# Four placings moved in a hand-ordered transformer block: values in their own unit, index pieces in four runs, a ring of four output weights, a nested loop for experts' further blocks

## The chip, the cores and the metric

The kernel runs on one core of one Trainium2 chip. The metric is the device time of one execution in microseconds (us). The engines are TensorE (PE in the profile, its weight loads PEld), VectorE (DVE), ScalarE (ACT), GpSimd (POOL) and SyncE (SP, which here only issues DMAs).

## What is computed

One layer of a streaming encoder over 1024 tokens of 1024 features, in float32. A mixer (an indexer that picks 256 keys for sparse attention, beside a forgetting attention), then a mixture of 32 experts, each behind an adaLN norm, then a last norm. Cut to what matters:

```python
x = x + gate1(c) * Mixers(adaLN(rmsnorm(x), c))
x = x + gate2(c) * HierMoE(adaLN(rmsnorm(x), c))
return rmsnorm(x, g_final)

# Mixers
rel   = einsum('bqhd,bsd->bqhs', qi_blk, ki) * IDX_SCALE        # index scores, 8 heads
score = einsum('bqh,bqhs->bqs', wi_blk, relu(rel)); sel = top_k(score, 256)
oa = softmax(q . k[sel]) . v[sel]                               # branch a, one shared key head
ob = softmax(q . k + cum_q - cum_k) . v                         # branch b, causal
merged = sigmoid(ga) * (oa @ w_out_a) + sigmoid(gb) * (ob @ w_out_b)
return merged @ w_out

# HierMoE: every token goes to 2 of 32 experts; an expert's tokens are padded to blocks of 128
hid = silu(xb @ w_e_gate[e]) * (xb @ w_e_up[e])                 # 1024 -> 512
y_block = hid @ w_e_down[e]                                     # 512 -> 1024
```

With the inputs of this case the 32 experts have, in the order in which the kernel takes them, 1,1,1,2,1,1,3,2,2,1,2,1,1,1,7,3,1,1,2,2,1,1,3,1,1,1,1,1,2,1,1,1 blocks: 51 in all. Here they are called expert 0 to expert 31 in that order.

## The kernel before

The program of each engine is written out by hand, in the order in which it runs; engines meet by semaphores only. The stages, with their place in the profiled execution: norms and the first projection (to 131 us), the index scores (131 to 206), the rest of the gate columns of that projection (206 to 545), 64 attention units (555 to 794), the output weights of the two branches (795 to 900), the merged projection, the second norm and the router (900 to 1050), the experts (1050 to 1773), the last norm (to 1809).

A product that needs more than one pass of rounded numbers is written as three matmuls (L1192, L1193, L1194), each operand being split into a rounded high part (by ACT) and what is left (by DVE).

Index scores: 24 pairs of heads' scores (L1186); ACT turns each score tile into its relu (`positive`, L891), DVE adds it to the block's sum (L1691, L1694) and thereby frees one of two relu buffers. Between the pairs PE does 32 pieces of the gate columns, three matmuls each, placed by the table `PIECE_AFTER` after 21 of the pairs, never more than four in a row. In the stage before, DVE has, at its steps t=6 and t=7, two `mod_sums` (L1547), which multiply rows of the modulation.

Attention: unit n is a pair of heads by a block of 128 queries. On PE a turn of the loop does `turn_p(n)` (transposes of unit n's probabilities, L1328), the scores of unit n+3 (L1315), and `values(n-1)` (L1340): the values of a unit come a turn behind its transposes. ACT copies the transposes out of the accumulators (`turned`, L943), which `values` waits for; DVE's `out` (L1790) copies the result out, takes the largest score (L1771) and scales (L1785).

Output weights: 16 units u, each 24 matmuls against a slice of `w_out_a` and `w_out_b`. SP loads the slice (L591), ACT rounds it (L953), DVE makes its rest (L1866) and merges the results (L1910, L1912). There are two buffers for the slices, and SP issues the load of slice u when PE is through with slice u-2.

Experts: `expert()` is written five times, once ahead of a loop, three times in it and once behind. The loop runs ten times over three experts; in this text place 1, 2 and 3 are the three experts of a turn, so that place 3 is followed by the loop's jump back (L1521). The number of an expert's blocks is read at run time: its first block stands unconditional, the second and third behind a compare-and-branch each (L1505, L1507), the rest behind a third (L1509). Behind that one there are two copies of the block's program, each within a loop: one for blocks 3 to 7, one for blocks 8 up. `MORE` is where the second begins. Expert 14 alone has more than three blocks.

Of the kernel before, what the change touches and what calls it, by code (L numbers as in the profile page):

```python
# [45 lines left out]
MORE = 8  # L46
# [27 lines left out]
PIECE_AFTER = [0, 0, 0, 0, 1, 1, 2, 2, 5, 6, 6, 7, 8, 9, 10, 10, 11, 12, 13, 13, 14, 15, 16, 16, 17, 18, 19, 19, 20, 21, 22, 22]  # L74
# [65 lines left out]
def build(nc, x, c, positions, w_mod, b_mod, g_mix, w_in, b_forget, w_out_a, w_out_b, w_out, g_ffn,  # L140
# [13 lines left out]
    with ExitStack() as ctx:  # L154
# [85 lines left out]
        relu = [at(30, U), at(31, U)]  # L240
# [65 lines left out]
        w_raw = [at(u, U) for u in (13, 28)]  # L306
        w_lo = [fr(u, U) for u in (13, 28)]
        w_hi = [fr(u, U) for u in (34, 35)]
# [71 lines left out]
        wo_in = [sem(f"wo_in{z}") for z in range(2)]  # L380
# [26 lines left out]
        sq2_ok = sem("sq2_ok")  # L407
        ms2_ok = sem("ms2_ok")
        sqrt2_ok = sem("sqrt2_ok")
# [101 lines left out]
        def _(sp):  # L511
# [44 lines left out]
            bias_rows(0)  # L556
            for j in range(2):
                sp.wait_ge(gate_ok, 2 * j + 2)
                gate_store(0, j)
            for s in GATE_SLOTS:  # L560
# [27 lines left out]
            def weights_o(u):  # L588
                m, z = u % KT, u % 2
# [15 lines left out]
            for u in range(2):  # L605
                weights_o(u)
# [3 lines left out]
            for u in range(4):  # L610
                gates_back(u)
            for u in range(2, N_G):
                if u >= 4:
                    sp.wait_ge(mg_done, 2 + u - 3)
                    gates_back(u)
                sp.wait_ge(yab_ps, u - 1)
                weights_o(u)
                if u == KT + 2:
                    weights_out(0)
# [36 lines left out]
            sp.wait_ge(sq2_ok, TT)  # L656
# [28 lines left out]
        def _(pool):  # L685
# [57 lines left out]
            pool.wait_ge(sq2_ok, TT)  # L743
# [60 lines left out]
        def _(act):  # L804
# [80 lines left out]
            def positive(n):  # L885
                w = WB[B0 + n // NH]
                act.wait_ge(rel_ps, n + 1)
                if n >= 2:
                    act.wait_ge(score_ok, n - 1)
                b = 2 * (n % 3)  # L890
                act.activation(relu[n % 2][:, 0:w], ps[:, b:b + 2, :].rearrange("p a b -> p (a b)")[:, 0:w], ACT.Relu,  # L891
# [59 lines left out]
            def high_w(u):  # L951
                act.wait_ge(wo_in[u % 2], 32 * (u // 2) + 32)
                act.activation(w_hi[u % 2], w_raw[u % 2], ACT.Copy).then_inc(whi_ok, 1)  # L953

            for n in range(N_IU):
                positive(n)
                for g in range(4):
                    if n == 2 * PIECE_AFTER[KT * g + KT - 1] + 1 + (g > 0):
                        gate_half(g)
                if n in (24, 26):  # L960
                    high_slot(1, (n - 24) // 2)
# [69 lines left out]
            for t in range(TT + 1):  # L1031
# [3 lines left out]
                if t < TT:  # L1035
                    act.wait_ge(x1_ok, 2 * t + 2)
                    if t >= 1:
                        act.wait_ge(sq2_ok, t)
                    act.activation(sqj, x1[t], ACT.Square, accum_out=ssq[:, t:t + 1]).then_inc(sq2_ok, 1)
                    act.wait_ge(ms2_ok, t + 1)  # L1040
                    act.activation(rstd[:, t:t + 1], ssq[:, t:t + 1], ACT.Sqrt).then_inc(sqrt2_ok, 1)
# [52 lines left out]
            for t in range(TT):  # L1094
                act.wait_ge(x_in[t], 48)
                if t >= 1:
                    act.wait_ge(sq2_ok, TT + t)
                act.activation(sqj, xf[t], ACT.Square, accum_out=ssq[:, t:t + 1]).then_inc(sq2_ok, 1)
                act.wait_ge(ms2_ok, TT + t + 1)
                act.activation(rstd[:, t:t + 1], ssq[:, t:t + 1], ACT.Sqrt).then_inc(sqrt2_ok, 1)  # L1100

        @block.tensor
        def _(pe):
# [116 lines left out]
            for k in range(SCORE_PAIRS):  # L1220
                index_scores(2 * k)
                for i, after in enumerate(PIECE_AFTER):
                    if after == k:
                        piece(i // KT, i % KT)
# [4 lines left out]
                if k == 3:  # L1229
# [130 lines left out]
            for n in range(-LEAD, N_U + 1):  # L1360
                groups = len(key_groups(n)) if 0 <= n < N_U else 0
# [8 lines left out]
                if n >= 1:  # L1370
                    for f in range(len(key_groups(n - 1))):
# [757 lines left out]
```

## Time and profile before

| | us |
|---|---|
| median of 3 runs | 1813.42 (1812.15 to 1817.22) |
| profiled execution | 1810.58, of it the span 1808.8 |
| experts, 1050 to 1773 | 723.0, PE busy 610.8 |
| output weights, 795.1 to 900.4 | 105.3, PE busy 93.7 |
| index scores, 131.4 to 206.1 | 74.7, PE busy 63.8, DVE busy 55.2 |
| attention, 555 to 794 | 239.0, PE busy 220.2 |

The page adds up busy time by engine and by line over the whole span. The waits and the timeline tell which idle time lies ahead of which line and what ended it; "issue" is idle time in which the engine waited for nothing that the profile shows. The chain of waits follows the end of the program back, so that idle time in it is time that the program is long by.

### The profile page before, as it was taken

Reading aid. Unit: us, or ns where it says so; the run is one execution under the profiler, and the core shown is the slowest. Engines: PE = TensorE matmul, PEld = TensorE weight load, DVE = VectorE, ACT = ScalarE, POOL = GpSimd, SP = SyncE. Lnnn points to the kernel's source line nnn. Section 1 sums busy time; section 2 is a strip of 40 time slices with the busy share of each in tenths; the row PEclk is TensorE's granted clock in tenths of the full one; section 3 lists DMA queues with packets and bytes.
Section 4 is the critical chain, followed back from the end, with each engine's and each line's share of the span. In section 5 each row is a group of like instructions: output and inputs, shape, how many; then the busy total and the mean of one; then the engine's idle time right before and its main releaser. Section 6 shows DMA issues by size and latency. Waiting matters only on the chain.

```text
span 1808.8 us, 23911 instructions
## 1 busy us (share of the span) xinstructions
PE 1573.7 (87%) x8440; PEld 946.8 (52%) x8441; DVE 846.9 (47%) x1981; ACT 504.7 (28%) x1011; POOL 206.9 (11%) x372
## 2 busy tenths in 40 slices
PE   6989999999999999989799578898969989696693
PEld 3554578898897666667688432333323323232231
DVE  6887877877796777856565611111101111010013
ACT  4335421122225767742312111111101111010012
POOL 1110000000001210000000022222212222221121
PEclk9999999999999999999999788999989999898896
DMA  9651023321110002025661689868892588868955
GB/s 356 222 185 60 24 86 101 94 59 47 47 47 24 25 2 82 1 82 183 199 215 70 259 334 370 343 229 297 312 359 56 172 300 319 337 220 324 405 206 192
DMA packets 122316, 327.68 MB, mean 181 GB/s; under 512 B 14814, under 2 KB 64006, under 8 KB 97570
## 3 DMA queue, kind: packets, MB, share of 16 engines
q1 hardware_dynamic: 110404, 308.36, 45.9%
q0 software_dynamic: 11744, 16.82, 4.3%
q8 instruction: 137, 2.24, 0.6%
q14 instruction: 31, 0.25, 0.0%
HBM read 301.74 MB, written 34.39 MB: 186 GB/s over the span
## 4 chain that ended last, share of the span: by engine, by line
PE 80%; issue 8%; DVE 7%; DMA 2%; ACT 2%; SPq 1%; POOL 0%; POOLq 0%; ACTq 0%; DVEq 0%
PE ps L1457 22%; PE ps L1192 10%; PE ps L1475 9%; PE ps L1194 9%; PE ps L1193 9%; PE ps L1315 3%; PE ps L1328 3%; PE ps L1150 3%; PE ps L1340 3%; DVE arena L1771 2%; PE ps L1186 2%; DMA arena<-in_w_mod_dram 1%; PE ps L1451 1%; PE ps L1153 1%; PE ps L1466 1%
## 5 line engine op out<-in xcount | busy, mean ns | idle before, releaser
L1457 PE MATMUL ps<-arena 128*64 128x512 f32 x1632 | 400.1, 635 | 112.9 <-issue 112.2
L1457 PEld LDWEIGHTS ps<-arena 128*64 128x64 f32 x1632 | 123.4, 145 | 346.5 <-issue 339.6
L2073 DVE TENSOR_TENSOR arena<-arena,ps 128x256 f32<-128x256 f32 x51 | 21.5, 421 | 532.1 <-ACT arena L1066 532.1
L1475 PE MATMUL ps<-arena 128*64 128x512 f32 x816 | 183.8, 592 | 0.6 <-DVE arena L2089 0.6
L1716 DVE TENSOR_SCALAR_CACHE_REDUCE arena<-arena,small 128x384 bf16<-128x384 f32 (+2 forms) x192 | 169.3, 942 | 0.0
L1070 ACT ACTIVATE arena<-ps 128x256 f32<-128x256 f32 x51 | 19.5, 383 | 441.6 <-PE ps L1466 441.6
L796 POOL DMA_INDIRECT sum_rows<-arena,ones x51 | 81.5, 1598 | 531.7 <-DVE arena L2089 508.6
L1192 PE MATMUL ps<-rounded_quad,rounded_pair 128*128 128x512 f32 x352 | 138.2, 393 | 2.5 <-ACT arena L891 2.5
L1194 PE MATMUL ps<-rounded_quad,rounded_pair 128*128 128x512 f32 x352 | 137.1, 390 | 0.0
L1193 PE MATMUL ps<-rounded_quad,rounded_pair 128*128 128x512 f32 x352 | 137.1, 390 | 0.0
L1771 DVE CUSTOM_DVE_ANT_0 arena<-ps,arena 128x896 f32<-128x896 f32 (+7 forms) x128 | 91.8, 755 | 66.6 <-PE ps L1315 66.0
L1475 PEld LDWEIGHTS ps<-arena 128*64 128x64 f32 x816 | 58.7, 137 | 116.5 <-issue 116.5
L1192 PE MATMUL ps<-rounded 128*128 128x512 f32 x256 | 103.8, 405 | 17.1 <-issue 11.5
L936 ACT ACTIVATE arena<-arena,small 128x896 f32<-128x896 f32 (+7 forms) x128 | 98.5, 774 | 57.7 <-DVE small L1771 57.2
L1193 PE MATMUL ps<-rounded 128*128 128x512 f32 x256 | 101.9, 398 | 0.0
L1194 PE MATMUL ps<-rounded 128*128 128x512 f32 x256 | 101.8, 398 | 0.0
L2089 DVE SCALAR_TENSOR_TENSOR arena<-ps,ones,arena 128x512 f32<-128x512 f32 x51 | 38.3, 751 | 115.8 <-PE ps L1475 115.8
L1315 PE MATMUL ps<-arena 64*128 64x512 f32 (+3 forms) x384 | 79.3, 517 | 7.1 <-DVE small L1771 7.0
L1328 PE MATMUL ps<-ident,arena 128*128 128x128 f32 x576 | 80.2, 280 | 4.3 <-ACT arena L943 3.5
L1340 PE MATMUL ps<-arena 128*64 128x128 f32 x1152 | 77.0, 278 | 7.2 <-DVE arena L1790 6.2
L737 POOL TENSOR_SCALAR_AFFINE_SELECT arena<-arena 128x128 f32<-128x128 f32 x64 | 24.8, 413 | 508.5 <-DVE small L1771 478.4
L943 ACT ACTIVATE arena<-ps 128x512 f32<-128x512 f32 (+1 forms) x160 | 77.8, 549 | 12.8 <-PE ps L1328 12.8
(313 smaller groups left out, 2426.3 us busy)
## 6 DMA issues: line engine op xcount, KB each, us to landing
arena<-in_w_e_up_dram SPq DMA_DIRECT2D x64, 1024.0 KB, 11.9
arena<-in_w_e_gate_dram SPq DMA_DIRECT2D x64, 1024.0 KB, 10.2
arena<-in_w_e_down_dram SPq DMA_DIRECT2D x32, 2048.0 KB, 9.3
arena<-in_w_mod_dram SPq DMA_DIRECT2D x12, 2048.0 KB, 8.7
plain_pair<-in_w_in_dram SPq DMA_DIRECT2D x30, 512.0 KB, 5.2
arena<-in_x_dram SPq DMA_DIRECT2D x16, 512.0 KB, 7.3
gate_rows<-arena SPq DMA_DIRECT2D x16, 512.0 KB, 2.8
arena<-gate_rows SPq DMA_DIRECT2D x32, 256.0 KB, 4.3
```

The lines of the kernel that those rows point to most:

```text
L796: pool.indirect_dma_start(y_q, bass.IndirectOffsetOnAxis(idx_s[q][:, 0:1], 0), ye[z], None, bounds_check=S * NT - 1, oob_is_err=False, com ...
L936: act.activation(buf, buf, ACT.Exp, bias=nmax[:, u:u + 1], scale=-1.0, accum_out=rs[:, u:u + 1]).then_inc(p_done, 1)
L1192: pe.matmul(out, w_h, a_h, start=first, stop=False)
L1193: pe.matmul(out, w_h, a_l, start=False, stop=False)
L1194: return pe.matmul(out, w_l, a_h, start=False, stop=last)
L1315: m = pe.matmul(ps[:, 2 * z + a // 512, 0:e - a], q[half, b * P:(b + 1) * P], k[half, a:e], start=True, stop=True)
L1328: m = pe.transpose(ps[:, turn_bank(k), (2 * i + z) * P:(2 * i + z + 1) * P], lg[n % 4][z][:, kb * P:(kb + 1) * P], ident[:])
L1340: m = pe.matmul(ps[z * HD:(z + 1) * HD, 6, 0:P], v, pT[k % PT][:, (2 * i + z) * P:(2 * i + z + 1) * P], start=kb == 0, stop=kb == b)
L1457: m = pe.matmul(ps[o * TB:(o + 1) * TB, 2, 0:2 * FQ].rearrange("p (j n) -> p j n", j=2), xT[:, k % NX, k // NX * TB:(k // NX + 1) * TB], w ...
L1475: m = pe.matmul(ps[o * TB:(o + 1) * TB, 5, 0:DQ], hidT[:, k % NH_T, k // NH_T * TB:(k // NH_T + 1) * TB], w_dn[c][:, k, o * DQ:(o + 1) * D ...
L1716: chain.up(dve.tensor_scalar(junk[b % 2][:, 0:WB[B0 + b]], scb[b], thr(b), None, op, ALU.add, accum_out=cnt[:, b:b + 1]))
L1771: dve.tensor_tensor_reduce(lg[n % 4][z][:, 0:w], ps[:, 2 * z:2 * z + 2, :].rearrange("p a n -> p (a n)")[:, 0:w], added, -1.0 if kind == " ...
```

## The change

It does these things:

- Attention: `values` of unit n come in unit n's own turn, behind the scores of unit n+3; DVE's `out` moves with them.
- Index scores: the 32 pieces stand in four runs of eight, after pairs 2, 9, 14 and 19. A third relu buffer. The two `mod_sums` stand between scores of this stage (after scores 5 and 19). Small steps (transposes of the cumulative sum, rounding of slot 1) come later in the stage, and SP's `bias_rows(0)` waits for the stage's end.
- Output weights: a ring of four buffers for slices. Slice 0 is loaded before the attention ends, 1 to 3 behind its last scores (before: slices 0 and 1 ahead of them), and slice u when PE is through with slice u-4.
- Experts: behind the third compare-and-branch one copy of the block's program in a nested loop in the place of two.
- Six semaphores become three, with counts that go on.

```diff
-MORE = 8
+MORE = 5
-PIECE_AFTER = [0, 0, 0, 0, 1, 1, 2, 2, 5, 6, 6, 7, 8, 9, 10, 10, 11, 12, 13, 13, 14, 15, 16, 16, 17, 18, 19, 19, 20, 21, 22, 22]
+PIECE_AFTER = (2, 9, 14, 19)
-        relu = [at(30, U), at(31, U)]
+        relu = [at(30, U), at(31, U), at(35, U)]
-        w_raw = [at(u, U) for u in (13, 28)]
-        w_lo = [fr(u, U) for u in (13, 28)]
-        w_hi = [fr(u, U) for u in (34, 35)]
+        w_raw = [at(u, U) for u in (13, 9, 12, 28)]
+        w_lo = [fr(u, U) for u in (13, 9, 12, 28)]
+        w_hi = [fr(u, U) for u in (14, 36, 34, 35)]
...
-            for u in range(2):
-                weights_o(u)
+            weights_o(0)
             for z in range(2):
                 sp.wait_ge(gate_out[z], 16 * KT)
             sp.wait_ge(lg_done, 2 * N_U)
             for u in range(4):
+                if u >= 1:
+                    weights_o(u)
                 gates_back(u)
-            for u in range(2, N_G):
-                if u >= 4:
-                    sp.wait_ge(mg_done, 2 + u - 3)
-                    gates_back(u)
-                sp.wait_ge(yab_ps, u - 1)
+            for u in range(4, N_G):
+                sp.wait_ge(yab_ps, u - 3)
                 weights_o(u)
+                sp.wait_ge(mg_done, 2 + u - 3)
+                gates_back(u)
...
             def positive(n):
                 act.wait_ge(rel_ps, n + 1)
-                if n >= 2:
-                    act.wait_ge(score_ok, n - 1)
+                if n == 2:
+                    act.wait_ge(k_spread, TT)
+                if n >= 3:
+                    act.wait_ge(score_ok, n - 2)
...
-                if n in (24, 26):
-                    high_slot(1, (n - 24) // 2)
+                if n in (33, 35):
+                    high_slot(1, (n - 33) // 2)
...
             for k in range(SCORE_PAIRS):
                 index_scores(2 * k)
-                for i, after in enumerate(PIECE_AFTER):
-                    if after == k:
-                        piece(i // KT, i % KT)
+                for g in range(4):
+                    if PIECE_AFTER[g] == k:
+                        for kt in range(KT):
+                            piece(g, kt)
...
-            for n in range(-LEAD, N_U + 1):
-                groups = len(key_groups(n)) if 0 <= n < N_U else 0
+            for n in range(-LEAD, N_U):
+                groups = len(key_groups(n)) if n >= 0 else 0
...
-                if n >= 1:
-                    for f in range(len(key_groups(n - 1))):
-                        values(n - 1, f)
+                for f in range(groups):
+                    values(n, f)
...
                 with pe.If(3 < blocks):
-                    with pe.Fori(3, MORE) as k:
-                        with pe.If(k < blocks):
-                            token_block(first + k, c, own)
-                    with pe.If(MORE < blocks):
-                        with pe.Fori(MORE, RUN) as k:
-                            with pe.If(k < blocks):
-                                token_block(first + k, c, own)
+                    with pe.Fori(0, (RUN - 3 + MORE - 1) // MORE) as far:
+                        with pe.If(3 + MORE * far < blocks):
+                            with pe.Fori(0, MORE) as k:
+                                with pe.If(3 + MORE * far + k < blocks):
+                                    token_block(first + 3 + MORE * far + k, c, own)
...
                 low_h(t)
-                mod_sums(4 + t)
+                if t < TT - 2:
+                    mod_sums(4 + t)
...
+                for g in range(2):
+                    if n == 2 * PIECE_AFTER[g] + 1:
+                        mod_sums(10 + g)
...
-            for n in range(-LEAD, N_U + 2):
-                if n >= 2:
-                    out(n - 2)
+            for n in range(-LEAD, N_U + 1):
+                if n >= 1:
+                    out(n - 1)
```

On PE, the end of an expert's program before, from the third compare-and-branch (L1509) to the end of the second copy of a block:

```order
L1509 COMPARE_AND_BRANCH
L1510 UNCONDITIONAL_BRANCH
L1511 COMPARE_AND_BRANCH
L1481 ISA
L1457 MATMUL ps<-arena 64x512 x8
L1466 MATMUL ps<-ident,arena 128x128 x2
L1448 REGISTER_ALU
L1451 MATMUL ps<-ident,arena 128x128 x4
L1457 MATMUL ps<-arena 64x512 x8
L1475 MATMUL ps<-arena 64x512 x8
L1511 UNCONDITIONAL_BRANCH
L1510 REGISTER_ALU
```

And after, where the same branch stands on L1509 again:

```order
L1509 COMPARE_AND_BRANCH
L1510 UNCONDITIONAL_BRANCH
L1510 ISA
L1511 COMPARE_AND_BRANCH
L1512 UNCONDITIONAL_BRANCH
L1512 ISA
L1513 COMPARE_AND_BRANCH
L1481 ISA
L1457 MATMUL ps<-arena 64x512 x8
L1466 MATMUL ps<-ident,arena 128x128 x2
L1448 REGISTER_ALU
L1451 MATMUL ps<-ident,arena 128x128 x4
```

Before, these rows are followed by a second copy of the block (L1515); after, by the ends of the two loops and the next expert's reads of its numbers (L1501). So the branch jumps over one copy, not two.

On PE, the turn of an attention unit before, with the transposes (L1328), the scores (L1315) and the values (L1340):

```order
L1328 MATMUL ps<-ident,arena 128x128 x12
L1315 MATMUL ps<-arena 128x512 x2
L1328 MATMUL ps<-ident,arena 128x128 x2
L1340 MATMUL ps<-arena 64x128 x16
L1328 MATMUL ps<-ident,arena 128x128 x12
L1315 MATMUL ps<-arena 128x384 x2
```

After, in the same place (L1329, L1316 and L1341 are the same lines, moved by one):

```order
L1329 MATMUL ps<-ident,arena 128x128 x12
L1316 MATMUL ps<-arena 128x512 x2
L1329 MATMUL ps<-ident,arena 128x128 x2
L1341 MATMUL ps<-arena 64x128 x14
L1329 MATMUL ps<-ident,arena 128x128 x12
L1316 MATMUL ps<-arena 128x384 x2
```

The 16 matmuls belong to the unit before, the 14 to the unit whose 14 transposes stand above them.

On SP, the loads of the output weights (L591) among the gates' (L597) before:

```order
L591 DMA arena<-in_w_out_a_dram 128x4x128
L591 DMA arena<-in_w_out_b_dram 128x4x128
L591 DMA arena<-in_w_out_a_dram 128x4x128
L591 DMA arena<-in_w_out_b_dram 128x4x128
L597 DMA arena<-gate_rows 128x512 x8
L591 DMA arena<-in_w_out_a_dram 128x4x128
```

After, each slice has its gates behind it:

```order
L589 DMA arena<-in_w_out_a_dram 128x4x128
L589 DMA arena<-in_w_out_b_dram 128x4x128
L595 DMA arena<-gate_rows 128x512 x2
L589 DMA arena<-in_w_out_a_dram 128x4x128
L589 DMA arena<-in_w_out_b_dram 128x4x128
L595 DMA arena<-gate_rows 128x512 x2
```

## Rows read from the trace of the kernel before

**Rows 1.** The page: the span of the profiled execution.

```profile
span 1808.8 us, 23911 instructions
```

**Rows 2.** Stretches: bounds, length, busy (x) of PE PEld DVE ACT POOL, clock, DMA share, GB/s.

```profile
1050.00:1773.00 723.00, 610.81 (x2736) 221.31 (x2736) 79.72 (x151) 92.11 (x205) 151.81 (x198) 0.94 0.76 281
795.10:900.40 105.30, 93.68 (x384) 74.45 (x384) 56.98 (x77) 28.52 (x41) 0.00 (x0) 0.95 0.54 170
131.40:206.10 74.70, 63.77 (x269) 32.58 (x269) 55.22 (x72) 44.77 (x63) 1.02 (x2) 0.93 0.14 41
555.00:794.00 239.00, 220.19 (x2096) 153.83 (x2095) 171.25 (x503) 174.10 (x414) 21.28 (x56) 1.00 0.11 34
240.00:480.00 240.00, 240.00 (x1240) 203.49 (x1239) 191.55 (x521) 47.85 (x62) 0.00 (x0) 1.00 0.24 71
```

**Rows 3.** Waits of PE, 1040 to 1790 us: total, times, longest.

```profile
PE ps L1457 <- issue: 112.2, 29, 11.8
```

**Rows 4.** The chain of waits, its pieces of idle time: start us, us, what.

```profile
1088.24 3.63 issue
...
1252.93 6.72 issue
...
1310.28 11.20 issue
...
1567.95 11.77 issue
...
1643.69 11.26 issue
...
1681.65 4.00 issue
...
1698.95 11.25 issue
```

**Rows 5.** Expert 12's branches on PE's queue: count, ns, start.

```profile
L1509 PEldq COMPARE_BRANCH  x1: 5482/5482/5482, 1306.5 to 1306.5; - x1
L1521 PEldq COMPARE_BRANCH  x1: 7347/7347/7347, 1312.2 to 1312.2; - x1
```

**Rows 6.** Timeline of PE: start, us, line, names, count, idle before.

```profile
1298.69 3.65 PE L1457 MATMUL ps<-arena 128*64 128x512 f32 x16 [2.24 <-issue]
1306.67 3.60 PE L1475 MATMUL ps<-arena 128*64 128x512 f32 x16
1321.48 4.97 PE L1457 MATMUL ps<-arena 128*64 128x512 f32 x16 [11.20 <-issue]
```

**Rows 7.** DMA queue of instructions, 240 to 480 us: packets, MB, share.

```profile
q8 instruction: 9, 0.15, 0.3%
```

**Rows 8.** Output weights, 795.1 to 900.4 us: a wait, groups by line, PE's timeline.

```profile
ACT rounded L953 <- DMA arena<-in_w_out_b_dram: 75.8, 14, 11.4
L1192 PE MATMUL ps<-rounded 128*128 128x512 f32 x128 | 52.5, 410 | 13.3 <-issue 11.5 <-DVE rounded L1866 1.7
L1866 DVE TENSOR_TENSOR rounded<-arena,rounded 128x1024 fp32r<-128x1024 f32 x15 | 18.4, 1225 | 33.3 <-ACT rounded L953 33.3
799.34 0.39 PE L1194 MATMUL ps<-rounded 128*128 128x512 f32 x1
...
801.63 0.39 PE L1192 MATMUL ps<-rounded 128*128 128x512 f32 x1
```

**Rows 9.** Index scores, 131.4 to 206.1 us: groups by line, DVE and PE.

```profile
L1694 DVE SCALAR_TENSOR_TENSOR arena<-arena,small 128x384 f32<-128x384 f32 (+5 forms) x42 | 40.0, 951 | 15.1 <-ACT arena L891 12.8
L1547 DVE SCALAR_TENSOR_TENSOR arena<-arena,small 128x512 f32<-128x512 f32 x8 | 6.0, 752 | 0.2
L1192 PE MATMUL ps<-rounded_quad,rounded 128*128 128x512 f32 x32 | 15.7, 491 | 5.8 <-DVE rounded L1635 5.8
```

**Rows 10.** Timeline of attention, unit 38's turn: start, us, engine, line.

```profile
699.16 0.49 PE L1315 MATMUL ps<-arena 64*128 64x128 f32 x4
...
700.13 1.34 ACT L943 ACTIVATE arena<-ps 128x512 f32<-128x512 f32 x3
```

## The prediction before the result

> **What bounds the kernel now.** I read four views, in this order. First the table of stretches [rows 2]. TensorE is what the whole span [rows 1] is made of: in the gate columns it is busy for all 240.00 us of 240.00, so nothing is to be had there. It is not busy all the time in four other stages, and the change touches exactly these: the experts (610.81 of 723.00 us), the output weights (93.68 of 105.30), the index scores (63.77 of 74.70) and the attention (220.19 of 239.00).
>
> Then PE's waits over the experts [rows 3]: 112.2 us in 29 gaps, all ahead of the first gate matmuls of an expert (L1457), and all "issue": no semaphore, no weights. The chain of waits holds these gaps, so the end is late by them. It also shows their size by place in the loop [rows 4]. At 1252.93, 1310.28, 1567.95, 1643.69 and 1698.95 us they are 6.72, 11.20, 11.77, 11.26 and 11.25 us: these five, 52.2 us, stand behind experts with one block at place 3, where the loop jumps back. The rows 3.63 and 4.00 are the first and the last of six at place 2 (20.7 us together). What is left, some 39 us, is small gaps at all places.
>
> The branches say what the gaps are made of. Behind expert 12 the third compare-and-branch takes 5.48 us and the loop's jump 7.35 us [rows 5]; the work that was queued ahead runs on for a part of that, and 11.20 us stay open. Such a branch costs little when it doesn't jump, so it is the fetch of instructions at the target that is paid. The first work behind a long gap is slow too: L1457's first half takes 4.97 us behind the gap of 11.20 and 3.65 us behind one of 2.24 [rows 6].
>
> Last the output weights [rows 8]: ACT waits 75.8 us for the slices' DMA, the slice of DVE's rest (L1866) waits for ACT, and PE has 13.3 us idle ahead of L1192.
>
> **Part D, the nested loop.** It takes one copy of a block out of what the third branch jumps over. How much is that? Nine packets of instructions came in 240 us [rows 7], for 1240 matmuls and 1239 weight loads [rows 2]: some 275 a packet. A block is 54 matmuls and 54 loads, 0.4 packet with its few others. The branch jumped over nearly a whole packet and jumps over half of one now; the turn of three experts shrinks from about 6.8 packets to 5.5. The rows don't show a jump over half a packet. The bounds: it costs as much as today's (nothing gained), or it falls within what is already there and costs nothing; then all that L1509 adds goes. I take half of the branch's 5.48 us, 2.7 us, since every second such jump then ends in a packet that the engine holds. For the jump back I take 7.35 less 2.7, by the same step, for the shorter way. So a long gap at place 3 loses 5.5 us: five times 5.5 is −27.5. At place 2 only the branch bears on it: the six gaps lose half, −10. Where gaps fall from 4 to 2 us the slow first half (4.97 against 3.65 [rows 6], 1.3 us each) goes as well, for some three of them: −4. The small gaps I leave. What stands next behind them is the weights: an expert's are 6.3 MB, and 281 GB/s at a share of 0.76 [rows 2] is 370 GB/s at full share, so 17.0 us an expert against 11.4 us of matmuls for one block (three pieces of 3.6 us as in [rows 6] and the turns between them); 51 blocks take 580 us, 32 experts' weights 545. Over the stage it holds, and three sets are loaded ahead, but strings of one-block experts eat that up. Sum D: −41, from 0 to −55.
>
> By a page of the Trainium skill, "Runtime: NRT & Kernel Launch", section "Instruction fetch mechanics", instructions come in blocks of 256, two of which are held, and a jump out of this window forces a fetch; by that a skip of about one block or of half of one would mostly fall inside, and the gaps at L1509 would not be there. The trace has 5.48 us on such a skip, so it pays well inside of two packets; taken by the rule alone, the shorter skip would bring nothing there, which is the rival of no gain below.
>
> **Part C, the ring of four.** Today SP asks for a slice when PE has done the one two before, so the slice has little over one unit's time (5.4 us: 24 matmuls by the pitch of 0.2267 us that the ten matmuls from 799.34 to 801.63 us show [rows 8]) to land, be rounded by ACT and by DVE (1.2 us). With four it has three units' time, 16 us. The stage then goes at that pitch: 384 by 0.2267 is 87.1 us against 105.3, −18. DVE has 57.0 us of work there [rows 2], no bound. But slice 1 to 3 are asked for only when the last scores are done, all at once beside gates, and land late for units 1 and 2; and the first matmuls stand at the lower clock (mean 0.95). I put +2 for that. Sum C: −16, from −12 to −17. In the last units of attention the earlier slice 1 is missing, but nothing reads it.
>
> **Part B, the index scores.** The pieces were a cover: PE did one or two of them while ACT and DVE worked a pair off. Eight in a row are 24 matmuls, 5.4 us and 0.4 of slower first ones: 5.8 us in which no score comes. The ring of three gives DVE three scores (3 by 0.951 us, 2.9) in them. So DVE stands 2.9 us in each of four runs, 11.6. It also gets 6.3 us more of work: `mod_sums` is 8 by 0.752 us [rows 9] and two now lie between scores, where one had its place at the stage's beginning. 55.2 plus 6.3 of work, 11.6 behind the runs and 8 us of today's 19.5 idle (74.7 less 55.2 [rows 2]) that I keep for the stage's start are 81.1 us, and I round up for the transposes, which now stand between scores too: 82 against 74.7, +7. DVE becomes the bound. Against it works that `mod_sums` covers the first two runs, that PE's wait of 5.8 us on L1635 [rows 9] at the start goes: then +1. If also the covers fail, +9. The stage before stays: PE bounds it. SP's `bias_rows(0)` behind the stage's end has the whole gate stage to land in: nothing.
>
> **Part A, values in their own unit.** Before, a turn lay between the transposes and the values; now only the scores of unit n+3 do. In unit 38's turn PE ends these scores at 699.65 us and ACT's copies of its transposes run to 701.47 [rows 10]: the values would stand 1.8 us. That is where the unit three ahead is short and the unit itself long, once or a little more in each eight units: 8 by 1.8 is 14.6. PE is idle for 18.8 us of the stage already (239.00 less 220.19 [rows 2]), and a wait put in takes half of another's place. So +7, from 0 (the waits only change places) to +15. `out` comes a turn earlier as well, and the stage's last turn is a unit shorter: below 0.5 us.
>
> The merged semaphores add and remove no instruction that waits longer: 0.
>
> **The sum.** Against the profiled execution's 1810.6: −41 −16 +7 +7 is −43, 1767.6. The median of the runs is 2.8 us over the profiled one: 1770.
>
> **Rivals.**
> (1) Only part of D comes. The gaps shorten, but now PE gets to experts before their weights: in strings of one-block experts 17.0 us of transfer stand against 11.4 of work. For it: DMA share 0.76 over the stage, near full in its strings. Against: today no wait of L1457 names a DMA of weight. Half of D, some 20 us, is lost: 1790. I give it 0.22.
> (2) More of D comes. The skip stays within what is held at nearly all places: −41 becomes −55, and the index stage loses only 2: 1751 to 1752. 0.10.
> (3) D brings nothing, since a jump costs a fetch whatever its length; the edit doesn't do in effect what its form says. −16 +7 +7 is −2: 1811. 0.11.
> (4) Slower. Where a jump lands in a packet decides what it costs, as the places show: 11 us at place 3, 2 to 4 at the others, for the same skip. The program's layout shifts, and behind the shorter skip the loops' ends and the next expert's reads fall on a packet's edge at place 2 and 1 as well. If eight gaps there rise from 3.4 to the 6.7 of the smallest long one [rows 4], that is +26, and with −2 for the rest 1835 to 1838. It decides from 0.3 us per gap on. 0.07.
> My forecast, 1760 to 1780, has 0.50.
>
> **The numbers.** Three tenths of a per cent, 5.4 us, is about what a measurement of this kernel can tell from no change. The forecast and rivals 1 and 2 are faster, and a third of rival 3: faster 0.84, within 0.3% 0.08, slower 0.08. The range: rivals 3 and 4, 0.18, are left out; it goes from rival 2's end to a little beyond rival 1, for the upper bound of A and B: 1748 to 1803.
>
> **What would show it.** In the changed kernel's profile: issue waits ahead of L1457 of 60 to 75 us in place of 112, the place-3 gaps near 6 us; L1509 about 2.7 us on the third branch. A wait of L1457 on a DMA of weights would be rival 1, L1509 as today rival 3. The output-weight stage should take 87 to 91 us, with no idle of L1192 but at its start. The index stage should end its scores near 213 us with DVE's L1694 idle behind ACT in four blocks of 3 us. In the attention L1340 should wait for ACT's copies, some 10 us in all. Wrong it is above all if the jumps' cost is not in proportion to what is jumped over.

## The result and the profile after

The changed kernel takes 1690.5 us, median of four runs (1687.4 to 1694.6), against 1815.3 us before: a ratio of 0.931, with a 95% interval of 0.929 to 0.934. It is 125 us faster. I had forecast 1770, in a range of 1748 to 1803, that is 43 us less: the direction was right and the size wrong by a factor of three. Span for span, the profiled executions are 1692.8 and 1808.8 us, 116 us apart. The kernel before was timed again beside each group of the runs below, with medians of 1814.3 to 1817.6 us, so a difference of some 3 us between runs of different groups tells little.

From the first and last instructions of TensorE's groups in both traces, the time went as follows.

| stretch | before | after | difference | forecast |
|---|---|---|---|---|
| to the first index score | 132.2 | 133.7 | +1.5 | 0 |
| index scores, to the first slot matmul (B) | 73.9 | 85.7 | +11.8 | +7 |
| gate columns | 326.5 | 328.2 | +1.6 | 0 |
| attention, to the first output-weight matmul (A) | 262.7 | 278.4 | +15.7 | +7 |
| output weights to the end of the router (C) | 223.1 | 205.2 | −17.9 | −16 |
| to the first gate matmul of an expert | 31.8 | 31.6 | −0.2 | 0 |
| experts (D) | 728.2 | 598.8 | −129.4 | −41 |
| rest | 30.6 | 31.3 | +0.8 | 0 |

So three of the terms are of the forecast's kind, and D is three times its size. The page of the changed kernel, its first lines and its queue of instructions, and then TensorE's waits from 1030 to 1680 us (total, times, longest):

```profile
span 1692.8 us, 23924 instructions
...
q8 instruction: 54, 0.88, 0.2%
```

```profile
PE ps L1457 <- issue: 9.7, 5, 4.1
...
PE ps L1457 <- DMA arena<-in_w_e_up_dram: 3.4, 2, 2.7
```

The 112.2 us of [rows 3] have become 9.7, in 5 gaps in the place of 29. The branches of the loop tell where they went. These are the views of the third branch and of the jump back (now L1519) from 1120 to 1640 us, that is from the end of the loop's first turn (count, ns as shortest, median and longest, first and last start):

```profile
L1509 PEldq COMPARE_BRANCH  x28: 68/202/210, 1120.7 to 1636.5; - x28
```

```profile
L1519 PEldq COMPARE_BRANCH  x10: 76/208/218, 1121.0 to 1636.9; - x10
```

In [rows 5] they were 5482 and 7347 ns, and the jump back over the whole loop was this before:

```profile
L1521 PEldq COMPARE_BRANCH  x10: 76/5348/7635, 1113.0 to 1760.3; - x10
```

Now no such branch takes over 0.22 us after the first turn, neither a skip nor the jump back over three experts' programs. And the queue of instructions carried 54 packets over the whole execution; before it carried 137:

```profile
q8 instruction: 137, 2.24, 0.6%
```

Of these, the experts' stage had 92 before and has 9 now. The 83 that are gone are, but for two, nine in each of the nine turns after the first: the whole loop was fetched anew in every turn, and now it is fetched once. This is the third of the ten turns before, 1184.6 to 1253.0 us; in the changed kernel the queue has no packet at all from 1125 to 1640 us, which is nearly all of the nine turns behind the first.

```profile
q8 instruction: 9, 0.15, 1.0%
```

That is not what I had costed, which was a skip's length.

The groups by line, L1457 before and after:

```profile
L1457 PE MATMUL ps<-arena 128*64 128x512 f32 x1632 | 400.1, 635 | 112.9 <-issue 112.2
```

```profile
L1457 PE MATMUL ps<-arena 128*64 128x512 f32 x1632 | 373.9, 600 | 13.7 <-issue 9.7 <-DMA arena<-in_w_e_up_dram 3.4 <-ACT arena L1062 0.7
```

The gaps gave 102.5 us (112.2 less 9.7) and the end of the slow first halves behind them (4.97 against 3.65 us in [rows 6]) another 26.2 (400.1 less 373.9): 128.7, nearly the whole of the stage's 129.4. The granted clock of the stage was 0.94 [rows 2] and is 0.99. Here are the experts, the output weights and the attention as stretches (length, busy and count of PE, PEld, DVE, ACT and POOL, clock, DMA share, GB/s):

```profile
1062.60:1661.50 598.90, 585.20 (x2754) 213.43 (x2754) 80.45 (x152) 92.46 (x207) 153.69 (x202) 0.99 0.88 337
825.90:912.70 86.80, 86.79 (x383) 71.89 (x384) 56.69 (x77) 28.26 (x41) 0.00 (x0) 1.00 0.66 206
547.50:825.90 278.40, 250.28 (x2257) 176.28 (x2257) 187.36 (x527) 187.07 (x431) 23.66 (x62) 0.98 0.11 33
```

### The profile page after: what moved, and what is told of

It is laid out like the page before. It is cut to its first block, busy times and chain, and to the rows that moved or that the text cites. A ratio compares the mean times of both kernels' runs of the same rounds, so it can differ in the third digit from the quotient of the medians.

```text
span 1692.8 us, 23924 instructions
## 1 busy us (share of the span) xinstructions
PE 1546.8 (91%) x8440; PEld 942.9 (56%) x8441; DVE 846.4 (50%) x1981; ACT 506.3 (30%) x1011; POOL 205.9 (12%) x372
## 4 chain that ended last, share of the span: by engine, by line
PE 81%; DVE 7%; DMA 4%; ACT 4%; issue 3%; SPq 1%; POOL 0%; POOLq 0%; ACTq 0%; DVEq 0%
PE ps L1457 20%; PE ps L1192 10%; PE ps L1194 10%; PE ps L1193 10%; PE ps L1475 10%; PE ps L1341 3%; PE ps L1150 3%; PE ps L1316 3%; PE ps L1329 3%; PE ps L1186 2%; DVE arena L1773 2%; DMA arena<-in_w_e_up_dram 2%; DMA arena<-in_w_mod_dram 2%; PE ps L1451 1%; ACT arena L936 1%
## 5 line engine op out<-in xcount | busy, mean ns | idle before, releaser
L1457 PE MATMUL ps<-arena 128*64 128x512 f32 x1632 | 373.9, 600 | 13.7 <-issue 9.7
L1457 PEld LDWEIGHTS ps<-arena 128*64 128x64 f32 x1632 | 113.9, 138 | 226.7 <-issue 215.5
L1475 PE MATMUL ps<-arena 128*64 128x512 f32 x816 | 183.8, 592 | 0.6 <-DVE arena L2091 0.6
L1475 PEld LDWEIGHTS ps<-arena 128*64 128x64 f32 x816 | 58.7, 137 | 116.5 <-issue 116.5
L1192 PE MATMUL ps<-rounded 128*128 128x512 f32 x256 | 101.2, 395 | 5.6 <-DVE rounded L1896 3.9
L1194 PE MATMUL ps<-rounded 128*128 128x512 f32 x256 | 100.3, 392 | 0.0
L1193 PE MATMUL ps<-rounded 128*128 128x512 f32 x256 | 100.1, 391 | 0.0
L1316 PE MATMUL ps<-arena 64*128 64x512 f32 (+3 forms) x384 | 81.3, 529 | 10.1 <-DVE small L1773 9.6
L1329 PE MATMUL ps<-ident,arena 128*128 128x128 f32 x576 | 82.8, 286 | 7.9 <-ACT arena L943 7.0
L1341 PE MATMUL ps<-arena 128*64 128x128 f32 x1152 | 79.7, 284 | 8.4 <-ACT arena L943 7.0
```

Source lines behind the costliest of these rows:

```text
L1192: pe.matmul(out, w_h, a_h, start=first, stop=False)
L1193: pe.matmul(out, w_h, a_l, start=False, stop=False)
L1194: return pe.matmul(out, w_l, a_h, start=False, stop=last)
L1316: m = pe.matmul(ps[:, 2 * z + a // 512, 0:e - a], q[half, b * P:(b + 1) * P], k[half, a:e], start=True, stop=True)
L1329: m = pe.transpose(ps[:, turn_bank(k), (2 * i + z) * P:(2 * i + z + 1) * P], lg[n % 4][z][:, kb * P:(kb + 1) * P], ident[:])
L1341: m = pe.matmul(ps[z * HD:(z + 1) * HD, 6, 0:P], v, pT[k % PT][:, (2 * i + z) * P:(2 * i + z + 1) * P], start=kb == 0, stop=kb == b)
```

## The experiments

My theories, made after the profile above: H, the engine holds a certain number of instruction packets, and a loop that lies in no more than these is fetched once; S, the prediction's, that a jump costs by its length. The positions given below are counted from the order of TensorE's program, in packets of 256 instructions. I put the error of the count at about two tenths of a packet; no view prints a position, but the number of packets that have come by the loop's first jump back tests it, below.

### Each part by itself

**The nested loop alone**, on the kernel before:

```diff
-                    with pe.Fori(3, MORE) as k:
-                        with pe.If(k < blocks):
-                            token_block(first + k, c, own)
-                    with pe.If(MORE < blocks):
-                        with pe.Fori(MORE, RUN) as k:
-                            ...
+                    with pe.Fori(0, (RUN - 3 + MORE - 1) // MORE) as far:
+                        with pe.If(3 + MORE * far < blocks):
+                            with pe.Fori(0, MORE) as k:
+                                ...
```

> The kernel before with the nested loop alone (one copy of a block behind the third branch in the place of two). Theory H, the loop of three experts is now held: its program, which was fetched again in each of the ten turns, is short enough to stay in the engine's instruction buffer, so the branches cost 0.2 us from the second turn on and the experts take 599 us as in the changed kernel, not 728: 129 us less, about 1684 us against 1813. Theory S, it is the length of the skip (my prediction's step): five long gaps lose 5.5 us and six at place 2 lose half, 1772 us. A third, that the ring or the order ahead of the experts helped them (weights earlier, other phase): then this edit alone gives less than 129 us, 1700 us or more.

Measured: 1684.1 us (1682.6 to 1689.6), ratio 0.930 (0.926 to 0.933), 54 instruction packets. The experts take 599.2 us. H's number was 1684; S's, 1772, falls. The waits of TensorE from 1030 to 1660 us:

```profile
PE ps L1457 <- issue: 10.2, 5, 4.0
```

By the medians this edit alone is 6 us faster than the whole change; the ranges of the two overlap, so this comparison by itself isn't clear of noise.

**The ring of four alone**, with the merged semaphores:

```diff
-        w_raw = [at(u, U) for u in (13, 28)]
+        w_raw = [at(u, U) for u in (13, 9, 12, 28)]
...
+                sp.wait_ge(yab_ps, u - 3)
                 weights_o(u)
```

> The kernel before with the ring of four output weights alone (and the merged semaphores, which it needs room for). If the stage's 18 us less in the changed kernel (first output-weight matmul to last router matmul, 223.1 to 205.2) are the ring's, this is 18 us faster than before, 1796 us, with issue gaps of the experts as before (112 us). If they lean on the later attention or its slower clock, less than 12 us.

Measured: 1798.1 us (1795.1 to 1808.2), ratio 0.991 (0.989 to 0.994), 16 us faster. Output weights to router: 206.8 us against 223.1. The gaps ahead of the experts' first gate matmuls (L1454 in this kernel) are as before:

```profile
PE ps L1454 <- issue: 113.4, 29, 11.4
```

ACT's wait for the slices, over the output-weight stage of this run:

```profile
ACT rounded L950 <- DMA arena<-in_w_out_b_dram: 49.8, 13, 10.8
```

It was 75.8 us [rows 8]. ACT still waits that long because it runs ahead, and TensorE no longer waits for it: in the changed kernel it is busy for 86.79 us of 86.80 in this stage, above.

**The attention's values back**, in the changed kernel:

```diff
-            for n in range(-LEAD, N_U):
+            for n in range(-LEAD, N_U + 1):
...
-                for f in range(groups):
-                    values(n, f)
+                if n >= 1:
+                    for f in range(len(key_groups(n - 1))):
+                        values(n - 1, f)
```

> The changed kernel with the values a turn behind their transposes again, as before. From first scores to first output-weight matmul the changed kernel takes 278.4 us, the kernel before 262.7. If the place of the values alone does that, this is 16 us faster than the changed kernel, 1675 us, the waits of values and transposes on ACT's copies (7.0 and 7.0 us) fall to 0 and 3.5 and the granted clock in the attention rises from 0.97 to 1.00. If the later loads of the output weights or the index stage had part in it, 8 us or less.

Measured: 1678.3 us (1676.3 to 1681.2), 12.3 us faster than the changed kernel, less than the 16 expected. The attention takes 264.2 us in place of 278.4. TensorE's waits in it, first of the changed kernel, then with the values back (L1316 scores, L1341 values, L1329 transposes):

```profile
PE ps L1316 <- DVE small L1773: 9.6, 12, 1.2
PE ps L1341 <- ACT arena L943: 7.0, 8, 1.3
PE ps L1329 <- ACT arena L943: 7.0, 8, 1.3
PE ps L1341 <- DVE arena L1792: 1.2, 3, 0.4
```

```profile
PE ps L1316 <- DVE small L1774: 7.0, 9, 1.0
PE ps L1341 <- DVE arena L1793: 6.2, 10, 2.0
PE ps L1329 <- ACT arena L943: 3.5, 5, 1.1
...
PE ps L1341 <- ACT arena L943: 0.7, 1, 0.7
```

The values wait for ACT's copies of the same unit's transposes, 6.3 us more; the transposes, which come behind them, wait 3.5 more, the scores 2.6 more; the wait for DVE's `out` is 5.0 less. That is 7.4 us. The rest is the matmuls themselves: TensorE's busy time in this stage is 250.3 us in the changed kernel and 244.0 with the values back, at a mean granted clock of 0.98 and 0.99. With the index stage also as before (below) it is 242.4 at 1.00. The lower clock stands beside more idle time; that it is caused by it, these runs don't separate.

**The index stage back**, in the changed kernel: all of the table of pieces, the relu buffers, the two sums and the steps' places.

```diff
-PIECE_AFTER = (2, 9, 14, 19)
+PIECE_AFTER = [0, 0, 0, 0, 1, 1, 2, 2, 5, 6, 6, 7, ...
...
-        relu = [at(30, U), at(31, U), at(35, U)]
+        relu = [at(30, U), at(31, U)]
```

> The changed kernel with the index stage as before: pieces after 21 pairs, two relu buffers, the two modulation sums ahead of the stage. The stage takes 85.7 us from first scores to first slot matmul in the changed kernel, 73.9 before. If the stage is cut off from the rest, this is 12 us faster than the changed kernel, 1679 us. If the gate stage behind it only waits less for something else now, 5 us or less.

Measured: 1678.2 us (1677.0 to 1678.8), 12.3 us faster. The stage takes 74.5 us.

**Both back**, so that the ring and the nested loop are left:

> The changed kernel with the attention's values and the index stage both as before: what is left of the change is the ring and the nested loop. If the two stages' losses add up, it is 28 us faster than the changed kernel, 1663 us, and 150 us faster than the kernel before.

Measured: 1666.1 us (1665.3 to 1668.1), ratio 0.917 (0.914 to 0.920). That is 24.4 us faster than the changed kernel, not 28; the 28 came from stretches of the traces. The two losses add up (24.6 by the two runs apart, 24.4 together). The four parts measured apart, −130.2, −16.2, +12.3 and +12.3, are −121.8; the whole change is −124.8.

### What the experts' loop costs by its size and place

Spare copies of a block's program were put behind the third branch. They need eight blocks to be run, and the most here are seven, so what is executed stays the same.

```diff
+                    if spare:
+                        with pe.If(RUN - 1 < blocks):
+                            token_block(first + RUN - 1, c, own)
```

> The changed kernel with one more copy of a block's program behind the third branch of the experts at place 1 and place 2, which never runs here (it needs eight blocks, the most here are seven). The skip there is as long as before; the loop is 6.5 packets of 256 instructions by my count of the program, and lies in 7 of them. Theory H (what counts is how many packets the loop lies in, against what the engine holds): all branches cost 0.2 us from the second turn on, 1691 us, no time lost. Theory S (length of the skip): places 1 and 2 lose as before, branches of 3 to 5.5 us, some 40 us lost, 1730 us.

> The same, with a third such copy behind expert 0, ahead of the loop. The loop and all its skips are the same as in the run with spare copies at places 1 and 2; only its start moves by 0.44 packet, so that it lies in 8 packets (47.76 to 54.27 by my count) in the place of 7. Theory H with the edge between 7 and 8: it is fetched again in each turn, 80 to 129 us lost, 1770 to 1820 us, some 80 more instruction packets. Theory S, and theory H with the edge by length alone: nothing changes, 1691 us.

> The changed kernel with a spare copy at all three places: the loop is 6.95 packets long, as before, and lies in 8. Theory H: as slow as before in the experts, about 129 us lost, 1820 us. Theory S: about as slow as its skips make it, which are those of before too, so also 1800 to 1820. This run tells whether the nested form itself has a part in the gain: if it had, this would stay below 1750 us.

> The changed kernel with a spare copy behind expert 0, ahead of the loop, and one at place 1. The loop starts where it did in the slow run with copies ahead and at places 1 and 2 (47.76 by my count), but is 6.1 packets long and lies in 7 (to 53.83). Theory H: as fast as the changed kernel, 1691 us, some 55 instruction packets. If the copy ahead itself or the loop's start made that run slow, and not the number of packets, this one is slow too: 80 us or more lost, 1770 us.

| kernel | loop from, to (packets, counted) | length | lies in | us | packets fetched |
|---|---|---|---|---|---|
| changed | 47.32, 52.95 | 5.6 | 6 | 1690.5 | 54 |
| spare at 1 and 2 | 47.32, 53.85 | 6.5 | 7 | 1693.0 | 55 |
| spare at 1, one ahead of the loop | 47.76, 53.84 | 6.1 | 7 | 1689.9 | 55 |
| spare at 1 and 2, one ahead | 47.76, 54.29 | 6.5 | 8 | 1823.2 | 136 |
| spare at 1, 2 and 3 | 47.32, 54.30 | 7.0 | 8 | 1813.1 | 136 |
| before | 47.76, 54.71 | 6.9 | 8 | 1815.3 | 137 |

The second and the fourth are the pair that decides. Their loops are the same, instruction for instruction, skips and all; only 0.44 packet of program that never runs has been put ahead of the loop. It costs 130 us. The waits from 1030 to 1800 us, with copies at 1 and 2, and with the one ahead as well:

```profile
PE ps L1457 <- issue: 10.2, 5, 4.1
```

```profile
PE ps L1457 <- issue: 112.5, 30, 11.4
```

The jump back in each (L1522), in the fast one and in the slow one:

```profile
L1522 PEldq COMPARE_BRANCH  x10: 76/208/219, 1118.2 to 1633.4; - x10
```

```profile
L1522 PEldq COMPARE_BRANCH  x10: 76/5330/7568, 1121.6 to 1768.8; - x10
```

S falls by the first run alone: with skips at places 1 and 2 as long as before, nothing is lost. That the copy ahead or the loop's start is to blame by itself falls by the last run. The spare copy at all three places, in the nested form, is as slow as the kernel before, so the nested form as such gives nothing. All six rows go by the number of packets in which the loop lies: 6 or 7 fast, 8 slow.

The traces bear the count out. These are the instruction packets from the start to the loop's first jump back, in the changed kernel (to 1121.0 us), with copies at 1 and 2 (to 1118.2), and with the one ahead as well (to 1121.6):

```profile
q8 instruction: 51, 0.84, 0.3%
```

```profile
q8 instruction: 52, 0.85, 0.3%
```

```profile
q8 instruction: 53, 0.87, 0.3%
```

With one copy at 1 and one ahead they are 52 too, in the kernel before and with all three copies 53: the engine gets to one packet more wherever the count has the loop end in one more. From then on the kernels whose loop lies in 8 fetch nine packets in each of the nine turns left, one more than the loop lies in; those whose loop lies in 6 or 7 fetch one right behind the first jump back and none in the other turns. And behind a jump back two come at once (before, 1184.6 to 1186 us):

```profile
q8 instruction: 2, 0.03, 14.3%
```

One rival is left: by the count all six loops begin in packet 47, so the rows go as well by where the loop ends (up to 53.85 fast, from 54.29 slow), and no run moved the beginning over an edge. The nine packets in each turn speak for the number, but don't prove it.

The Trainium skill, page "Runtime: NRT & Kernel Launch", section "Instruction fetch mechanics", gives TensorE a memory of 2048 instructions, filled in blocks of 256, which is eight blocks; the runs agree, if one of the eight is taken by the block that is fetched ahead of the running one. The nine packets a turn and the two at once fit that, but no run here separates it from another use of the eighth. The same section's window of two pages for jumps, from which my prediction argued, does not agree: jumps over 0.5 to 6.5 packets take 0.2 us where the loop lies in 6 or 7 packets.

### What the index stage loses by

**The two sums ahead of the stage again**, pieces in runs of eight:

```diff
-                if t < TT - 2:
-                    mod_sums(4 + t)
+                mod_sums(4 + t)
```

> The changed kernel with the two modulation sums ahead of the index stage again (12.6 us of VectorE's work); the pieces stay in four runs of eight. The index stage takes 85.7 us from first scores to first slot matmul in the changed kernel, 73.9 before. Theory V (VectorE is the bound of the stage, my prediction's sum): most of the 12 us go with the sums, though PE then waits 5.8 us for them at the start as before: 76 to 79 us, 7 to 9 us faster than the changed kernel. Theory R (the runs of eight leave ACT and VectorE with nothing): at most 3 us faster.

Measured: 1693.3 us (1688.5 to 1693.8), no gain over 1690.5 and no loss clear of noise; the stage takes 88.6 us, not less than 85.7. Of the 3 us more, 1.6 are a longer wait for VectorE's L1678 near the stage's start (7.4 us against 5.8), and TensorE's mean granted clock is 0.89 against 0.94. VectorE's idle time ahead of its scores rises from 15.9 to 28.3 us instead. This is its row in the run with the sums ahead:

```profile
L1692 DVE SCALAR_TENSOR_TENSOR arena<-arena,small 128x384 f32<-128x384 f32 (+5 forms) x41 | 38.6, 942 | 28.3 <-ACT arena L891 25.7 <-DVE arena L1692 0.5
```

Theory V, my sum, falls: VectorE has 12 us less to do and the stage is no shorter. TensorE's wait for ACT's relus is the same as in the changed kernel (it was 1.1 us in the kernel before):

```profile
PE ps L1186 <- ACT arena L891: 15.5, 17, 1.6
```

**The pieces after 21 pairs again**, sums and three buffers kept (the transposes of the cumulative sum go back to their earlier place with them):

```diff
-                for g in range(4):
-                    if PIECE_AFTER[g] == k:
-                        for kt in range(KT):
-                            piece(g, kt)
+                for i, after in enumerate(PIECE_AFTER):
+                    if after == k:
+                        piece(i // KT, i % KT)
...
-                if n == 11:
+                if n == 7:
```

> The changed kernel with the pieces after 21 of the pairs again, never over four in a row; the two modulation sums stay between the scores, the three relu buffers too. Theory R: the stage falls to 74 to 78 us, 8 to 12 us faster than the changed kernel. Theory V: VectorE's work (60 us and its unavoidable waits at the start) still is there, but the 11.6 us that it stood behind the runs go: some 78 us. If both have to be there for the loss, both this and the run with the sums back are over 6 us faster.

Measured: 1687.1 us (1682.9 to 1690.1), 3.4 us faster, with ranges that overlap; the stage takes 82.0 us. Less than R said. TensorE now stands 3.8 us for VectorE's transposed sums, which the spread table needs early and which now lie behind one of the two modulation sums, and 4.7 us for ACT. Its granted clock is 0.89 on average against 0.94, and its busy time 69.8 us against 62.3. So each half of the edit hinders when it stands by itself (88.6 us with the runs of eight alone, 82.0 with the sums alone, 85.7 with both), and only with both undone does the stage come to 74.5 us. The parts don't add up, and what the third buffer and the small steps do in the stage with eight in a row was not measured apart.

What bounds the stage is seen in TensorE's timeline, first of the changed kernel, then of the one before, for pairs of the same size:

```profile
206.05 1.99 PE L1186 MATMUL ps<-arena 64*128 64x512 f32 x8
209.14 1.99 PE L1186 MATMUL ps<-arena 64*128 64x512 f32 x8 [1.11 <-ACT arena L891]
212.24 1.99 PE L1186 MATMUL ps<-arena 64*128 64x512 f32 x8 [1.11 <-ACT arena L891]
```

```profile
191.82 1.99 PE L1186 MATMUL ps<-arena 64*128 64x512 f32 x8
...
194.91 1.99 PE L1186 MATMUL ps<-arena 64*128 64x512 f32 x8 [0.21 <-ACT arena L891]
...
198.01 1.99 PE L1186 MATMUL ps<-arena 64*128 64x512 f32 x8 [0.21 <-ACT arena L891]
```

The pairs start every 3.1 us in both. A pair needs the accumulator that the first of the two relus of the pair ahead frees, so pair and relu go one behind the other (1.99 and 0.97 us; the two relus behind the pair of 206.05 are this row):

```profile
208.07 1.94 ACT L891 ACTIVATE arena<-ps 128x1024 f32<-128x1024 f32 x2 [5.85 <-PE ps L1186]
```

Before, a piece of 0.7 us lay in the gap and cost nothing; now the gap is empty and the pieces come on top. TensorE's waits for the relus, over the stage of the changed kernel and over that of the kernel before:

```profile
PE ps L1186 <- ACT arena L891: 15.5, 17, 1.6
```

```profile
PE ps L1186 <- ACT arena L891: 1.1, 3, 0.7
```

**A third relu buffer on the best kernel:**

> Ring of four and nested loop with the attention and the order of the index stage as before (1666.1 us so far), and of the index edits only the third relu buffer, with the bias rows' load behind the stage that makes room for it. PE waits in that stage 1 to 2 us for relu buffers as it is, so nothing: 1664 to 1667 us. If ACT's relus hold the stage there, up to 3 us faster.

Measured: 1665.6 us (1664.3 to 1666.7) against 1666.1: nothing, as expected. This and the run with both back are the fastest kernels here, 24 to 25 us ahead of the changed one.

## Why the prediction was wrong, and where it was right

- **D, −41 forecast, −130 measured (alone −130.2).** The reading of the profile was right: idle time before L1457 with no releaser, in the chain, made of branches that wait for instructions, with the slow first halves behind. The step that failed is the one on the price of a jump: I took "half of the branch's 5.48 us" for half the length of the skip, that is a cost in proportion to length. The cost hangs on whether the loop is still held: 0.2 us at each branch where it is, and 5.3 us in the median at the jump back where it is not. The forecast said itself that it would be wrong above all there. The trace of before had the sign of it: 92 packets came in the experts' stage, nine for each turn, and a loop that is seven packets long and lies in eight can't draw as many unless it is fetched anew each turn. I had counted the loop (6.8 packets before, 5.5 after; 6.9 and 5.6 by the tables above) and not asked what size can be held.
- The bound of −55 stood for all that the third branch adds, and its working isn't written out; the gaps at places 3 and 2 are 72.9 us together, so it left out a part even of these. The small gaps "that I leave", some 39 us, went as well but for 9.7 us in all, and so did the slow halves, 26 us where I had 4.
- **Rival 1** (weights late in strings of one-block experts) is there but small: two waits, 3.4 us together, at a DMA share of 0.88. My 17.0 us for an expert's weights is 544 us for all, under the 599 that the stage now takes.
- **Rivals 3 and 4** were the right question with the wrong half: a loop's place in the packets can decide over 130 us. The copy ahead of the loop shows that to be so. In the change as made it had no part: 5.6 packets lie in six or seven wherever they begin, and both are fast here.
- **C, −16 forecast, −17.9 in the trace, −16.2 alone:** right, by the pitch and 384 matmuls. The stage came to 86.8 us (87.1 forecast as its floor), so the +2 for late slices was not needed. The two rows named for the pitch give 2.29 us for ten matmuls, 0.229 each and 87.9 us in all; the 0.2267 I took is nearer to what the stage has, 86.8 for 384.
- **B, +7 forecast, +12 measured.** The direction was right, by the wrong engine. I made VectorE the bound and summed its work; taking 12 us of it away changed nothing. It was TensorE behind ACT's relus: 17 waits, 15.5 us, against 1.1 before. The last scores ended at 217.3 us, where 213 was forecast. The 3.1 us pitch with pieces inside stood in the timeline of before, and I had not read it as a floor that the pieces didn't raise. The term missed: eight pieces in a run cost what they take, 5.4 us each run, less what they still cover; four runs would be some 22 us by this, of which 12 are seen as loss, and how much the covers are worth was argued, not measured.
- **A, +7 forecast, within 0 to 15; +12.3 measured (11 to 16 in the traces).** The mechanism is as forecast, the size at the upper part: the waits gave 7.4, near my 7, and 6 us of slower matmuls came on top, which the sum had no term for.

## What to carry to other kernels

In these runs a run-time loop was either held by the engine or fetched again in every turn, and one packet more or less in which it lay made the difference: count the loop's instructions and where it begins, look at the instruction queue's packets per turn and at the durations of the compare-and-branches before costing any single jump. If packets still come in every turn, about as many as the loop lies in, shorten the loop, or move its start, until they stop; a rarely used second copy of a body is the first to take out. And work that stands between two steps of a ping-pong chain (matmul, relu, matmul) is free only there: gathering it in long runs turns it into time.

## What the runs showed of the hardware that I had not expected

- The edge is sharp, and lies between loops counted to end at 53.85 and at 54.29 packets. Loops in 6 and 7 packets: 54 and 55 packets fetched, 1690 to 1693 us. In 8: 136 or 137 packets, 1813 to 1823 us. Moving the same loop by 0.44 packet of code that is never executed costs 130 us.
- Once held, a jump's cost does not depend on its length: 202 ns in the median for the third branch, in the changed kernel (a skip of half a packet) as with spare copies at two of three places (nearly a whole one), 208 ns for the jump back over 5.6 or 6.5 packets.
- Fetching is dearer than its transfers: the 92 packets took 1.0% of the DMA engines' time in the experts' stage, and the stage lost 129 us by them.
